# Five more in-projection slabs by seven products: paced fillers for the value and gate slabs, and the convolution's second gate slab behind the gate columns

## The reference

```python
h = rmsnorm(x, g1)
q, k_cmp, v_cmp, k_sel, v_sel, k_win, v_win, gate_pre, \
    mq, mk, mv, mo, mi, mf, cab = split(h @ w_in, IN_SPLITS)   # w_in: 2048 x 5688
nsa   = nsa_attention(...)          # softmax scores with ALiBi, three branches, gated
ml    = mlstm(mq, mk, mv, mi, mf) * sigmoid(mo)
conv  = conformer(cab)              # a * sigmoid(gate), 31 taps, layernorm, silu
x = x + concat(nsa, ml, conv) @ w_out
x = x + moe(rmsnorm(x, g2))         # 4 groups of 8 experts, best group, top 2 in it, hidden 512
return rmsnorm(x, g3)
```

## Time and profile before

| | |
|---|---|
| median of 3 runs | 1427.34 us (1425.18 to 1428.28) |
| the profiled execution's own time | 1428.03 us |
| its span in the trace | 1426.2 us |
| mean granted PE clock | 0.943 of full speed |
| PE busy | 1205.7 us (85%) |
| DVE / ACT / POOL busy | 483.6 / 255.3 / 13.5 us |
| HBM traffic | 476.05 MB read, 335 GB/s over the span |

### The profile page before, as it was taken

How to read it: one execution, slowest core, us unless ns; L and a number is a source line. 1 busy time by engine, 2 the same in 40 slices (tenths; PEclk the granted TensorE clock), 3 DMA queues, 4 the chain that set the end, 5 groups by cost and what they waited for, 6 DMA issues and landing times.

```text
span 1426.2 us, 17903 instructions
## 1 busy us (share of the span) xinstructions
PE 1205.7 (85%) x7431; PEld 708.9 (50%) x7431; DVE 483.6 (34%) x1001; ACT 255.3 (18%) x629; POOL 13.5 (1%) x82
## 2 busy tenths in 40 slices
PE   8999999999999998669689958768587695876977
PEld 7999999766568753123244314224142241422422
DVE  5398997663875431121110220111101111011123
ACT  2101111444600122011111101002020010201112
POOL 2000000000010000000000000000000000000000
PEclk9999999999999999889999989989899898998989
DMA  9958677431644899999999999999999999999995
GB/s 318 274 158 194 167 161 236 119 82 38 165 112 166 346 413 426 429 427 427 428 428 428 426 428 427 427 427 429 428 426 427 429 427 425 431 426 426 429 427 237
DMA packets 133362, 479.34 MB, mean 336 GB/s; under 512 B 47804, under 2 KB 105632, under 8 KB 107552
## 3 DMA queue, kind: packets, MB, share of 16 engines
q1 hardware_dynamic: 126816, 477.58, 85.9%
q10 hardware_dynamic: 6464, 0.58, 0.4%
HBM read 476.05 MB, written 2.10 MB: 335 GB/s over the span
## 4 chain that ended last, share of the span: by engine, by line
PE 52%; DMA 43%; ACTq 2%; DVE 1%; ACT 1%; issue 1%; DVEq 0%
DMA ring<-in_expert_w_up_dram 36%; PE PS L1127 13%; PE PS L1447 10%; DMA spare<-in_expert_w_up_dram 6%; PE PS L1269 5%; PE PS L1169 3%; PE PS L1434 3%; PE PS L1246 2%; PE PS L1638 2%; ACTq L1862 2%; PE PS L1425 1%; PE PS L1221 1%; PE PS L1119 1%; PE PS L1648 1%; PE PS L1188 1%; PE PS L1509 1%
## 5 line engine op out<-in xcount | busy, mean ns | idle before, releaser
L1447 PE MATMUL PS<-ring,XG 128*32 128x512 f32 x1296 | 222.2, 734 | 147.9 <-DMA ring<-in_expert_w_up_dram 107.3
L1447 PEld LDWEIGHTS PS<-ring,XG 128*32 128x32 f32 x1296 | 57.6, 131 | 274.9 <-issue 271.8
L3068 DVE TENSOR_TENSOR hTe<-PS,sg 128x128 f32<-128x128 f32 (+1 forms) x31 | 9.9, 320 | 349.3 <-ACT sg L2193 349.1
L2885 DVE TENSOR_TENSOR x<-PS,x 128x1024 f32<-128x1024 f32 x41 | 50.2, 1225 | 209.8 <-PE PS L1526 208.4
L2181 ACT ACTIVATE Hs<-PS 128x512 f32<-128x512 f32 x30 | 17.9, 597 | 463.1 <-PE PS L1447 349.8
L1434 PE MATMUL PS<-ring,XG 128*64 128x512 f32 x192 | 84.6, 594 | 18.0 <-DMA ring<-in_expert_w_up_dram 14.5
L1526 PE MATMUL PS<-Y,SW 128*128 128x512 f32 (+2 forms) x176 | 90.6, 627 | 1.5 <-ACT ro L2289 1.5
L1447 PE MATMUL PS<-spare,XG 128*32 128x512 f32 x208 | 66.0, 793 | 27.8 <-DMA ring<-in_expert_w_up_dram 27.8
L1436 PE MATMUL PS<-ring,XG 128*64 128x512 f32 x192 | 85.0, 595 | 0.0
L1425 PEld LDWEIGHTS PS<-sel,xn 128*128 128x128 f32 x640 | 75.3, 191 | 13.0 <-issue 12.7
L1425 PE MATMUL PS<-sel,xn 128*128 128x128 f32 x640 | 77.6, 280 | 1.4 <-DVE x L2885 1.4
(11 more groups left out here) (494 smaller groups left out, 1577.2 us busy)
## 6 DMA issues: line engine op xcount, KB each, us to landing
ring<-in_expert_w_up_dram SPq DMA_DIRECT2D x53, 2048.0 KB, 23.8
ring<-in_expert_w_gate_dram SPq DMA_DIRECT2D x53, 2048.0 KB, 26.9
ring<-in_expert_w_down_dram SPq DMA_DIRECT2D x51, 2048.0 KB, 27.1
ring<-in_w_in_dram SPq DMA_DIRECT2D x17, 2048.0 KB, 9.5
spare<-in_expert_w_gate_dram SPq DMA_DIRECT2D x9, 2048.0 KB, 26.2
spare<-in_expert_w_up_dram SPq DMA_DIRECT2D x8, 2048.0 KB, 23.9
spare<-in_expert_w_down_dram SPq DMA_DIRECT2D x8, 2048.0 KB, 27.3
ring<-in_w_in_dram SPq DMA_DIRECT2D x16, 512.0 KB, 7.3
```

The lines of the kernel that those rows point to most:

```text
L1447: mm = pe.matmul(PS[r:r + 32, 0, :], gathered_rows(q, 4 * c + j)[:, column:column + 32], weight_rows(slots[u], 4 * (c % 2) + j), start=(c ...
L2885: dve.tensor_tensor(y, new, old, ALU.add).then_inc(sc_added, 1)
```

## The change

Five slabs turn fast, and the order around them moves.

1. **Early.** `small` moves from the ninth place to the second. cg1, so far plain and second, turns fast and stands third. The turning of parameters (`turn_params`) moves from behind cg1 to behind small, and ACT's loads of the router's weights (`load_router`, 12 DMAs) behind ACT's saves of cg.
2. **Late.** mv0, mv1, mo0 and mo1 turn fast: 4 x 56 = 224 filler steps of 128x128 in place of 128 of 128x256, in the order m2, m1, m6, m7, m5, m3, m4. The four weight sums of mv0 are DVE's (`first_late_sums`, ahead of biases(0)); those of the other three are POOL's (`late_sums_of`, 12 operations). DVE puts the products together (`late_first`, `late_last`, 4 operations each per slab), in place of eight saves of ACT.
3. **Ring.** The second score buffer, which was in x, and the new sums take ring slots 1 and 2; the out-projection's slots turn accordingly.

The core of the diff:

```diff
-SLABS = ["cg0", "cg1", "ca0", "ca1", "mq0", "mq1", "mk0", "mk1", "small", "kc0", "vc0", "ks0", "kw0",
+SLABS = ["cg0", "small", "cg1", "ca0", "ca1", "mq0", "mq1", "mk0", "mk1", "kc0", "vc0", "ks0", "kw0",
...
-FAST_SLABS = ("ca0", "ca1", "mq0", "mq1", "mk0", "mk1", "vc0", "ks0", "kw0", "vs0", "q0", "q1", "q2", "q3", "vw0")
+FAST_SLABS = ("cg1", "ca0", "ca1", "mq0", "mq1", "mk0", "mk1", "vc0", "ks0", "kw0", "vs0", "q0", "q1", "q2", "q3", "vw0",
+              "mv0", "mv1", "mo0", "mo1")
...
+LATE_SLABS = [u for u in FAST if u >= LATE]
+FAST_LATE = len(FAST) - len(LATE_SLABS)
+LATE_PRODUCTS = ["m2", "m1", "m6", "m7", "m5", "m3", "m4"]
+LATE_STEPS = 8 * len(LATE_PRODUCTS) * len(LATE_SLABS)
+SCALED = 2 + FAST_LATE
+LATE_SAVED = SCALED + 2 * len(LATE_SLABS)
...
-OUT_SLOTS = [(1, 2), (3, 4), (0, 5), (1, 2)]
+OUT_SLOTS = [(3, 4), (5, 0), (1, 2), (3, 4)]
...
-CHUNK_SLOT = [3, 4, 0, 5, 1, 2]
+CHUNK_SLOT = [5, 0, 1, 2, 3, 4]
...
-              for tile in (att[:, :], x1[:, :, :].rearrange("p t d -> p (t d)"))]
+              for tile in (att[:, :], ring[:, 1, :, :].rearrange("p k n -> p (k n)"))]
...
+        late_sums = ring[:, 2, :, :].rearrange("p k n -> p (k n)").rearrange("p (s a k n) -> p s a k n", s=2, a=2, k=8)
+        late_a, late_b = upto[:, :], cmask[:, :]
+        def late_part(name):
+            q = LATE_PRODUCTS.index(name)
+            return PS[:, q // 4, P * (q % 4):P * (q % 4) + P]
...
+            def late_sums_of(i):
+                j, u = FAST_LATE + i, LATE_SLABS[i]
+                n = UNITS[u][0]
+                pool.wait_ge(w_loaded[n % RING], slab_at[n])
+                pool.wait_ge(w_summed, 4 * j)
+                if i > 1:
+                    pool.wait_ge(unit_done, LATE_SLABS[i - 2] + 2)
+                pool.tensor_tensor(late_sums[:, i % 2, 0], quarter(u, 1, 1), quarter(u, 0, 1), ALU.subtract)\
+                    .then_inc(w_summed, 1)
+                pool.wait_ge(w_summed, 4 * j + 1)
+                pool.tensor_tensor(quarter(u, 0, 1), quarter(u, 0, 1), quarter(u, 0, 0), ALU.subtract)\
+                    .then_inc(w_summed, 1)
+                pool.wait_ge(w_summed, 4 * j + 2)
+                pool.tensor_tensor(late_sums[:, i % 2, 1], quarter(u, 1, 1), quarter(u, 0, 1), ALU.subtract)\
+                    .then_inc(w_summed, 1)
+                pool.wait_ge(prod_done, 2 * j + 1)
+                pool.wait_ge(w_summed, 4 * j + 3)
+                pool.tensor_tensor(quarter(u, 1, 0), quarter(u, 1, 0), late_sums[:, i % 2, 1], ALU.subtract)\
+                    .then_inc(w_summed, 1)
+            for i in range(1, len(LATE_SLABS)):
+                late_sums_of(i)
...
-                if u == 3:
+                if u == 2:
...
+                i, r = divmod(late[0], 8 * len(LATE_PRODUCTS))
+                name, k = LATE_PRODUCTS[r // 8], r % 8
+                j, u = FAST_LATE + i, LATE_SLABS[i]
+                n = UNITS[u][0]
                 if k == 0:
-                    pe.wait_ge(w_loaded[n % RING], slab_at[n])
-                    pe.wait_ge(unit_saved, LATE - 2 if u == LATE else u - 1)
-                mm = pe.matmul(PS[:, unit_bank(u), 0:256], hT[:, k, i * P:(i + 1) * P], ring[:, n % RING, k, :],
-                               start=(k == 0), stop=(k == DK - 1))
-                if k == DK - 1:
+                    if name == "m2":
+                        pe.wait_ge(w_loaded[n % RING], slab_at[n])
+                    if name == "m2":
+                        pe.wait_ge(first_scaled if i else unit_saved, SCALED + 2 * i - 1 if i else LATE - 2)
+                    if name == "m5":
+                        pe.wait_ge(first_scaled if i else unit_saved, SCALED + 2 * i if i else LATE)
+                    if name in ("m6", "m4"):
+                        pe.wait_ge(w_summed, 4 * j + {"m6": 3, "m4": 4}[name])
+                tokens, weights = {"m1": (tok_11, quarter(u, 0, 0)), "m2": (tok_12, quarter(u, 1, 0)),
+                                   "m3": (tok_s4, quarter(u, 1, 1)), "m4": (tok_22, quarter(u, 1, 0)),
+                                   "m5": (tok_s1, quarter(u, 0, 1)), "m6": (tok_s2, late_sums[:, i % 2, 1]),
+                                   "m7": (tok_s3, late_sums[:, i % 2, 0])}[name]
+                mm = pe.matmul(late_part(name), tokens[:, k], weights[:, k], start=(k == 0), stop=(k == 7))
+                if k == 7 and name in ("m2", "m7"):
+                    mm.then_inc(prod_done, 1)
+                if k == 7 and name in ("m3", "m4"):
                     mm.then_inc(unit_done, 1)
                 late[0] += 1
...
-            fill(8)
+            fill(16)
             pe.wait_ge(unit_saved, LATE)
             pe.wait_ge(cmp_saved, 1)
-            scores(0, 2)
-            scores(1, 3)
-            fill(16)
+            scores(0, 6)
+            scores(1, 6)
+            fill(28)
             pe.wait_ge(sT_ready, ML_H)
-            attend(0, 4)
+            attend(0, 5)
             scores(2, 3)
-            attend(1, 4)
+            attend(1, 5)
             mean_square(0)
-            scores(3, 3)
+            scores(3, 5)
             fill(LATE_STEPS)
             mlstm_values()
             pe.wait_ge(conv_out, CT)
-            pe.wait_ge(unit_saved, len(UNITS))
+            pe.wait_ge(first_scaled, LATE_SAVED)
...
+                if u == units_with("cg") - 1:
+                    load_router()
...
-            exponents(0, 0)
-            late_saves(1)
-            exponents(1, 1)
-            late_saves(2)
-            attend_saves(0, 1)
-            exponents(2, 0)
-            late_saves(1)
-            attend_saves(1, 1)
+            exponents(0)
+            exponents(1)
+            attend_saves(0)
+            exponents(2)
+            attend_saves(1)
             head_root(0)
-            exponents(3, 0)
-            late_saves(1)
-            act.wait_ge(unit_saved, len(UNITS))
+            exponents(3)
...
+            def first_late_sums():
+                j, u = FAST_LATE, LATE_SLABS[0]
+                n = UNITS[u][0]
+                dve.wait_ge(w_loaded[n % RING], slab_at[n])
+                dve.wait_ge(unit_done, LATE)
+                dve.tensor_tensor(late_sums[:, 0, 0], quarter(u, 1, 1), quarter(u, 0, 1), ALU.subtract).then_inc(w_summed, 1)
+                dve.wait_ge(w_summed, 4 * j + 1)
+                dve.tensor_tensor(quarter(u, 0, 1), quarter(u, 0, 1), quarter(u, 0, 0), ALU.subtract).then_inc(w_summed, 1)
+                dve.wait_ge(w_summed, 4 * j + 2)
+                dve.tensor_tensor(late_sums[:, 0, 1], quarter(u, 1, 1), quarter(u, 0, 1), ALU.subtract).then_inc(w_summed, 1)
+                dve.wait_ge(prod_done, 2 * j + 1)
+                dve.wait_ge(w_summed, 4 * j + 3)
+                dve.tensor_tensor(quarter(u, 1, 0), quarter(u, 1, 0), late_sums[:, 0, 1], ALU.subtract).then_inc(w_summed, 1)
+            def late_first(i):
+                _, part, _, s, _ = UNITS[LATE_SLABS[i]]
+                dst, c = mv if part == "mv" else mo, 256 * s
+                dve.wait_ge(prod_done, 2 * (FAST_LATE + i) + 2)
+                step(dve.tensor_copy(late_a, late_part("m1")))
+                issued(dve.tensor_tensor(dst[:, 0, c:c + P], late_part("m2"), late_a, ALU.add))
+                step(dve.tensor_tensor(late_a, late_part("m6"), late_a, ALU.add))
+                dve.tensor_tensor(late_b, late_part("m7"), late_a, ALU.add).then_inc(first_scaled, 1)
+            def late_last(i):
+                u = LATE_SLABS[i]
+                _, part, _, s, _ = UNITS[u]
+                dst, c = mv if part == "mv" else mo, 256 * s
+                dve.wait_ge(unit_done, u + 2)
+                dve.wait_ge(first_scaled, SCALED + 2 * i + 1)
+                both = issued(dve.tensor_tensor(late_a, late_part("m5"), late_a, ALU.add))
+                issued(dve.tensor_tensor(dst[:, 1, c:c + P], late_part("m4"), late_b, ALU.add))
+                issued(dve.tensor_tensor(dst[:, 1, c + P:c + 2 * P], late_part("m5"), late_b, ALU.add))
+                dve.wait_ge(dve_step, both)
+                dve.tensor_tensor(dst[:, 0, c + P:c + 2 * P], late_part("m3"), late_a, ALU.add).then_inc(first_scaled, 1)
+            first_late_sums()
+            biases(0, slab=0)
+            late_last(0)
+            biases(1, slab=1)
             gated(0)
+            late_last(1)
             gated(1)
+            late_first(2)
             biases(2)
+            late_last(2)
             head_squares(0)
             gated(2)
+            late_first(3)
             biases(3)
+            late_last(3)
             head_norm(0)
```

More of the change, by code:

```diff
@@ L177, in projection_units @@
         elif part == "kc":
-            units += [(n, part, "columns", s, 0), (n - 1, "small", "folded", 0, 0), (n, part, "columns", s, 1)]
+            units += [(n, part, "columns", s, 0), (n, "small", "folded", 0, 0), (n, part, "columns", s, 1)]
         elif part in ("mv", "mo", "vs", "vw"):
@@ L282 @@
               after("vw", 1): ["mlstm_turn"]}
```

(71 more changed lines are left out.)

42 lines of the change are left out of this document (21 added, 21 removed).

## The result

The change made the kernel slower: 1435.74 us (median of 6, 1433.12 to 1438.79) against 1426.55 before (here the median of 6 runs as well); the ratio is 1.0065, 95% interval 1.0053 to 1.0078, some 9 us. The forecast was 1423.1 with a range of 1420 to 1433. The rival C stood at 1434.8. The profiled execution has a span of 1437.0 against 1426.2; it took 1438.70, 3.0 above its median, and that of before 1428.03, 1.5 above, so the profiles differ by 10.8 us where the medians differ by 9.2.

What follows compares the result with a forecast made beforehand. The mixer on PE, then the expert stream at its DMA ceiling, were taken as the bound, mixer gains passing on one to one. Early -2.1 and late -2.1 gave -4.2, so 1423.1 us, range 1420 to 1433.

Steps and rivals of the forecast that it cites:

- rival C: In gated(0), POOL's four sums alternate with DVE's multiplications and hold them: +7.5 us, 1434.8 us, chance 0.16.
- case A: In the late part, DVE and POOL hardly hold each other: -4.2 us, 1423.1 us, chance 0.42.
- B: One POOL sum holds DVE at the end of scores(0), one holds gated(0): total 0, 1427.3 us, chance 0.24.
- early part: Start of the mixer, with small moved second and cg1 turned fast: -2.1 us, cg1's load staying hidden.
- nothing changes: From the last pair of scores(1) to attend(0), DVE's chain still ends last and stays at 9.13 us.
- the IOTA: POOL operation at 414.64 taking 0.48 us for 0.127, read as one engine waiting for the other's whole instruction.
- biases(0) +1.1: DVE's four first sums ahead of biases(0) make it start 1.1 us later.
- period of 2.17 us in scores(0): Each pair with six new filler steps takes 2.17 us for 1.80; seven pairs add 2.8 us.
- late_last(0) +0.3: Between the ninth and tenth pair, four operations from PSUM go in ahead of biases(1): +0.3 us.
- attend(0) -3.15: In attend(0)'s five blocks, 25 new filler steps replace 20 old ones: -3.15 us.
- scores(2): Three periods of 2.15 us fall only to 1.8, kept there by the handshake with DVE: -1.05 us.
- attend(1): First block gives only -0.2 us because PE waits for ACT's copy; the other four give -2.5 us.

Runs made afterwards that it cites:

- e1: The changed kernel with three added POOL waits that delay the fourth sums of the last three late slabs; 1423.5 us, ratio to before 0.9968.
- e4: The changed kernel with each of POOL's twelve sums cut to 512 of 1024 columns; 1429.55 us, ratio 1.0018.
- e5: The changed kernel with forty unread 128x128 products added on PE ahead of attend(0); 1433.47 us, ratio 1.0048.
- e2: The kernel before with only the early part: cg1 fast, small second, parameter turning and router loads moved; 1425.35 us, ratio 0.9987.
- e7: The changed kernel with POOL's twelve sums replaced by memsets of the same size; 1426.07 us, ratio 0.9996.
- e6: The changed kernel with gated(0)'s 16 multiplications as one operation with two SBUF operands; 1430.78 us, ratio 1.0033.

## Why the prediction was wrong

**The step that failed** is the choice of case A, that "DVE and POOL hardly hold each other", at 0.42 against 0.24 and 0.16 for B and C. The sum placed the meeting rightly (POOL from 308 to 318 and the multiplications at 308.4, both without the early part's -2.1; in the profile 309.64 to 319.46, and 312.07 behind the held product at 309.80), named the mechanism and priced C at +7.5 us; the change came out at +9.2. In the sum the same step is the sentence "nothing changes" between the last pair of scores(1) and attend(0), taken at 9.13 us: measured 17.57, of which 8.45 are DVE's held time, and 9.13 again in e1, where the sums are set aside.

C's working was 4 sums in gated(0) and 1.7 us in scores(0), 11.7 us; measured 8.45 + 1.55 = 10.0, of which all goes when the sums are set aside (e1) and half with half of the sums (e4). I judged that DVE's sixteen instructions might follow without a gap and leave POOL no turn. They leave one after each: a multiplication of 0.27 us, then a sum of POOL's, until POOL has no more.

No row of before could decide that. The prediction takes the IOTA for the only place where POOL and DVE are both at it in SBUF, but there is a second:

```profile
413.20 0.78 POOL L882 COPY hTe<-ident 36x36 f32<-36x36 f32 x2
413.28 0.62 DVE L2750 COPY xn<-x 128x512 f32<-128x512 f32 x1
```

Two equal copies of POOL take 0.78 us where larger ones take 0.226 each, and the second ends at 413.98, just behind DVE's copy (413.90). It is of the same kind as the first place: POOL waits, for one long DVE instruction.

Nor did the range follow from the rivals. It ended at 1433 and was said to leave out "the far end of C", but C's own value, 1434.8 at a chance of 0.16, lay outside it.

**What C lacked** is the clock. A wait of PE of 9.08 us costs 2.6 us more behind it (e5). In the profiled execution the wait of 2.28 us at 290.58 was followed by 1.5 us more (3.68 us to the eleventh pair for 2.17). Neither was in any case. That C's 1434.8 lies so near to the measured 1435.74 is in part luck: its blocked time is 1.7 us too long, and the clock's price is missing. Its sign, multiplications of 12 us or more, wasn't met either (10.69), since the first of the four sums held the product ahead of them. With the measured terms the sum is -4.2 + 10.0 + 2.6 + 1.5 = 9.9, against 10.1 in the profiles from the end of cg0 to the second mean square.

**The terms that held.** The early part, -2.1, measured -2.3 (e2), with cg1's load in time. biases(0) +1.1, measured 0.95. The period of 2.17 us in scores(0): measured 2.17 to 2.19 but for one of 2.51, and seven periods 15.57 for 15.4. The six of scores(1) take 13.40 for 13.2 in e1, which has no wait over 0.8 us there. late_last(0) +0.3: e1's tenth pair comes 2.99 us behind the ninth, where before has 2.67. attend(0) -3.15: with the clock up (e5) 15.92 us against 18.95, -3.03. scores(3) and late_last(3) to 0.1. The stream of experts passes it on, within the 3.4 us by which its length differs between profiles. A POOL sum was taken as 2.5 us and is 2.36.

**Smaller misses.** scores(2) gave -1.78 for -1.05: I counted three periods, and the fillers behind the fourth pair shrink as well (2.06 us from it to attend(1) before, 1.43 after). attend(1) gave 1.87 for its 2.7; POOL's last sum meets the small minimum of step 2 there (1.21 us at 349.57 in the chain of after), which I had not looked for.

Case A was right as arithmetic: with only waits of POOL added, which remove the meetings, e1 stands at 0.9968, or -4.6 us (-3.0 to -6.1), where A had -4.2. Its trace has the second mean square at 367.63, 3.58 earlier from a start 0.67 later, -4.25.

The port rule stands in the Trainium skill (SBUF — State Buffer, "Who interferes with whom"). By it DVE's second pair of SBUF ports is POOL's as well. Outside the two-port forms, which use both pairs for one input, a DVE instruction with at most one SBUF input doesn't meet POOL; one with two SBUF inputs meets POOL's instructions that read SBUF and not those that only write; an instruction in a two-port form, which a multiplication by a scalar can take, meets POOL in any case; and the issue order decides who waits. These runs agree. DVE's bias operations, one operand of which is in PSUM, stay at 0.41 us while POOL sums:

```profile
269.75 2.35 POOL L901 TENSOR_TENSOR ring<-ring 128x1024 f32<-128x1024 f32 x1 [259.20 <-DVE ring L2746]
270.00 0.41 DVE L2657 SCALAR_TENSOR_TENSOR spare<-dist,PS 128x256 f32<-128x256 f32 x1
```

The product of two SBUF operands is held by sums and not by a memset (e7), and the multiplications are held by either; that fits the two-port form, though no row names the form. For the order e6 agrees: POOL's sum begins 0.06 us behind DVE's operation and waits. Where the two rows begin within 0.04 us of each other, as at 314.70 and 314.71 in the change, the trace can't tell who was first. The prediction had the rule and the meeting, and gave them too little weight against one reason that it had not tested.

## What to carry to other kernels

An engine that looks idle is not free: here POOL's sums cost DVE 10.0 us and PE's clock some more. Before work is given to POOL, lay its instructions over DVE's in time. Count each one that meets a DVE operation with two SBUF operands, or a multiplication or minimum by a scalar from SBUF to SBUF, however small (128x8 here), at its full length. Then hang a wait on it that moves it to where DVE reads PSUM or stands idle, as e1 does. A chain of short operations lost a turn to each of POOL's sums here, and the long wait of PE was paid a second time in its clock.
